# Two chained transformer blocks on one core: pipelined heads and TensorE squares in the first, earlier gates, a first sparse score and a last projection by halves in the second

## The chip, the cores and the metric

The kernel runs on one core of a Trainium2 chip. The metric is the device time of one execution in microseconds (us), lower is better. Before the change three runs took 2322.05, 2326.41 and 2326.66 us, median 2326.41. The engines are TensorE (PE in the profile), ScalarE (ACT), VectorE (DVE), GpSimd (POOL) and SyncE (SP), each with its own queue in program order; they meet at semaphores.

## The reference

256 tokens of width 1024 pass through two layers of a first block and then two layers of a second block, all in fp32.

```
first block, each of 2 layers:
  h = rms_norm(x); one projection h @ w_in gives
    an LRU branch (conv, two sigmoid gates, a scan over time, gelu),
    8 heads of forgetting attention (fox), 4 heads of retention (rotary q and k, decay, norm)
  x += rms_norm(concat(lru, fox, ret) @ w_out)
  x += rms_norm(cross_attention(rms_norm(x), memory))      # 4 heads
  x += rms_norm(swiglu(rms_norm(x)))                        # hidden 2816
second block, each of 2 layers:
  x += 0.5 * swiglu(rms_norm(x))
  h = rms_norm(x); h @ w_in gives
    8 heads of sparse attention (NSA: compressed, selected, window, gated by sigmoid(24 logits)),
    4 heads of stick-breaking attention, 4 heads of window attention with sinks,
    3 x 1024 branch gates
  x += (sum of 3 gated branches) @ w_out
  x += 0.5 * swiglu(rms_norm(x))
```

## The kernel before

**Weights.** All weights come as one stream of 664 half slots of 128 x 1024 fp32 (512 KB), two per slot of 1024 x 256. SyncE loads a half into one of 4 ring buffers `raw`; ScalarE rounds it to fp32r (`w_hi`, L837, in `split_hi`); VectorE takes the rest (`w_lo`, L1351, in `split_lo`). `ahead(name)` in the programs of ScalarE and VectorE splits the slot that follows `name` in the stream; where it stands among the other work of that engine decides when the slot is ready. TensorE multiplies a half with `products` (L286): for each 128 x 128 tile three matmuls of 256 columns (hi x hi, hi x lo, lo x hi), so 24 a half and 48 a slot. After its last matmul a half raises `half_used`, which frees the ring buffer.

**Norms.** `norm_in` takes the new x by four pairs of 128-row tiles. For pair b VectorE updates x (`update`: L1409 twice, then L1413, x + sq), ScalarE makes `xn_hi` (L855, L856) and the square of x (L848), VectorE makes `xn_lo` (L1373). GpSimd adds the squares of pairs 1, 2 and 3 onto pair 0 (`add_squares`, L1964); when the sum is there TensorE makes the mean (`mean_square`, L335, two matmuls that show as 4 instructions). The slot that follows (`fed`) starts with the pairs that are there. There are five such norms, before cross attention and swiglu in both layers of the first block and before the first swiglu of the second block, beside others.

**First block, mixer.** TensorE runs the projections; the slot `f` gives 8 forget logits, from which ScalarE and VectorE compute their sums over time (`f8`; L1518 to L1528). TensorE turns them into biases (L415), then runs `rv`. GpSimd makes the angles, and ScalarE the sine after `ly` and the cosine (L934) after `f` (layer 0 only). Then `conv` (L1543, L1548), the LRU gates (L432), eight memory slots `ck0` to `cv3` (keys and values of cross attention), placed between: the LRU chain (L984 to L1574), rotary (L439, L1585 to L1588), the loop over fox heads (`fox_scores` L451, `fox_softmax` L1600 to L1466, `fox_turn` L363, `fox_values` L358, L359) and retention (L482, L1626, L490 on). In `fox_softmax` VectorE waits for the exponentials of ScalarE (L1008, L1009) inside each head. Retention does one head after the other: scores, decay, values. Then four slots `wo`.

**Second block.** After the projections TensorE runs 18 fill matmuls (`keep_busy`, L294), 24 gate logits as 16 matmuls of 24 columns (L652), `cmp_turn` (L601), the slot `sv` (`project(9)`), `cmp_out_of(1)` (L614), `stick_scores` 0 and 1, and the loop over NSA heads (L696 to L727): each step has scores, one slot of the branch gates (`bg`), turn and values. ScalarE makes the gates' sigmoid (L1208) after the slot `sv`. At the end four slots `up` give three branches by four column pairs; VectorE multiplies and adds them (L1919 to L1924), and gives `merged_hi` and `merged_lo` for pair b (L1329, L1361). After 24 fill matmuls the four slots `wo0` to `wo3` follow, one column pair each over all 8 row tiles; `add` (L1932) adds a finished pair, from PSUM, to x.

The order of the work is written out by hand in the five programs; nothing plans it.

Of the kernel before, what the change touches and what calls it, by code (L numbers as in the profile page):

```python
# [15 lines left out]
P = 128  # L16
D = 1024
KT = D // P
S = 256
# [80 lines left out]
def build(nc, A):  # L100
# [7 lines left out]
    def sb_at(name, shape, dt, offset):  # L108
# [85 lines left out]
    gate24 = stat[:, 4:6, 0:24]  # L194

# [55 lines left out]
    kc_mean, kc_root, kc_normed, gate_made, gate_ready, gates_out = (  # L251
        sig(n) for n in ("kc_mean", "kc_root", "kc_normed", "gate_made", "gate_ready", "gates_out"))
# [16 lines left out]

    def norm_no(L, k, add=False):  # L270

        n = 1 + 6 * L + 2 * k + add if L < DEPTH else 1 + 6 * DEPTH + 3 * (L - DEPTH) + k
        return n if n > 1 else 0

    added = [norm_no(L, k, True) for L in range(DEPTH) for k in range(3)]

    def sums_before(n):

        return 3 * n - len([a for a in added if a < n])


    def tensor_program():
# [22 lines left out]
        def slot_T(name, out, hi, lo, cts=(0, 1), fed=None, second=None):  # L305

            for half, r in halves(name):
                if half and second:
                    T.wait_ge(*second)
                if fed is not None:  # L310
                    for k in range(HK):
                        if k % 2 == 0:
                            T.wait_ge(*in_lo.at(4 * fed + 2 * half + k // 2 + 1))
                        for ct in cts:
                            m = products(out[:, ct, :], tile(r, k, slice(ct * P, (ct + 1) * P)),
                                         [t[:, half * HK + k, :] for t in (hi, lo)], half == 0 and k == 0 and ct == cts[0])
                else:
# [4 lines left out]
                m.then_inc(*half_used.next())  # L322

        def slot_rows(name, out, hi, lo):
            for half, r in halves(name):
                for rt in range(ST):
# [39 lines left out]
        def ffn(f, fed, n):  # L366
            slot_T((f, "gate", 0), dense[0], xn_hi, xn_lo, fed=fed)
            norm_scale(n)
# [21 lines left out]
        for L in range(DEPTH):  # L390
# [75 lines left out]
            for n in range(8 + 2):  # L466
# [11 lines left out]
            for h in range(4):  # L478
                q, k = lru_a[head_rows(h), h // 2, :], lru_t[head_rows(h), h // 2, :]
                b = flat(acc[h % 2])  # L480
                T.wait_ge(*(ret_decayed.at(4 * L + h - 1) if h >= 2 else scores_read.at(head + 8)))
# [4 lines left out]
                T.wait_ge(*ret_decayed.at(4 * L + h + 1))  # L486
                causal_values(acc[2 + h // 2][head_rows(h), 0, :], lambda kt: proj[:, 12, kt, h * HD:(h + 1) * HD],
                              probT[h % 2][:, 0, :]).then_inc(*ret_values.next())
# [14 lines left out]
            for n in range(4):  # L503
                T.wait_ge(*(cross_out.at(4 * L + n - 1) if n >= 2 else kv_out.at(8 * L + 7 + n)))
                slot_T(at(f"cq{n}"), dense[n % 2], xn_hi, xn_lo, fed=3 * L + 1 if n == 0 else None)
                if n == 0:
                    norm_scale(norm_no(L, 1))
# [46 lines left out]
        for L in range(DEPTH, 2 * DEPTH):  # L554
# [4 lines left out]
            def project(n, form=slot_T):  # L559
# [7 lines left out]
                form(at(("nq0", "nq1", "nk", "nc", "sq", "sk", "wq", None, "nv", "sv")[n]), dense[n % 2], xn_hi, xn_lo)  # L567
# [78 lines left out]
            keep_busy(18, mix_rows.at(3 * l + 1), dense[1])  # L646
            T.wait_ge(*wg_ready.at(l + 1))
            T.wait_ge(*head_root.at(5 * l + 5))
            wg = small_2("w_gate").rearrange("p (k n) -> p k n", k=KT)
            for rt in range(2):  # L650
                for k in range(KT):
                    m = T.matmul(bank[4][:, rt * 24:(rt + 1) * 24], x[:, k, rt * P:(rt + 1) * P], wg[:, k, :],  # L652
                                 start=k == 0, stop=k == KT - 1)
# [28 lines left out]
            stick_scores(1)  # L682
            T.wait_ge(*kc_normed.at(l + 1))
            T.wait_ge(*cmp_out.at(2 * l + 2))
            T.wait_ge(*gate_ready.at(l + 1))
            T.wait_ge(*head_normed.at(5 * l + 5))

            def nsa_scores(h):
# [3 lines left out]
                if h >= 1:  # L692
                    T.wait_ge(*scores_read.at(head + h))
                for b in range(2):
# [8 lines left out]
            def nsa_turn(h):  # L703
                lg = logit[h % 2]
                T.wait_ge(*probs_made.at(head + h + 1))
                if h >= 1:
                    T.wait_ge(*probT_made.at(head + h))
                    T.wait_ge(*probT_made2.at(8 * l + h))
                for b in range(2):
# [4 lines left out]
            def nsa_values(h):  # L714
# [6 lines left out]
                if h >= 1:  # L721
                    T.wait_ge(*y_made.at(16 + 12 * l + h))
                for b in range(2):
# [5 lines left out]

            slot = 0  # L730
            for n in range(8 + 2):
                if n < 8:
                    nsa_scores(n)
                if n not in (0, 6, 9):
                    gate_slot(slot)
                    slot += 1
                elif n:
# [91 lines left out]
    def scalar_program():  # L829
# [86 lines left out]
        def memory_step(name):  # L916
# [14 lines left out]
            elif name in ("ly", "f"):  # L931
                n = ("ly", "f").index(name)
# [3 lines left out]
        for L in range(DEPTH):  # L936
# [20 lines left out]
            AC.wait_ge(*f_read.at(L + 1))  # L957
            AC.activation(f8[:, 1, :], f8[:, 0, :], ACT.Abs, bias=small[0:8, SM1["fox_b"]]).then_inc(*f_abs.next())
            AC.wait_ge(*f_abs.last())
            AC.activation(f8[:, 1, :], f8[:, 1, :], ACT.Exp, scale=-1.0).then_inc(*f_exp.next())  # L960
            AC.wait_ge(*f_exp.last())
# [1260 lines left out]
```

## Time and profile before

| what | value |
|---|---|
| median of 3 runs | 2326.41 us (2322.05 to 2326.66) |
| profiled execution | 2324.44 us, its span 2323.1 us |
| mean granted TensorE clock | 0.973 |
| PE busy | 2197.7 us, 95% of the span |
| DVE, ACT, POOL busy | 1419.0, 1131.7, 91.0 us |
| HBM traffic | 360.36 MB, mean 155 GB/s |

A time read in the profile is from the span's start. Busy time of PE is modelled, so that 95% doesn't mean that TensorE runs at its peak. In the views of waits, a row names the instruction that waited and what ended the wait. In the chain, each piece ends by releasing the next one.

### The profile page before, as it was taken

The numbers are of one execution on the slowest core, as the hardware profiler recorded it, in microseconds if no ns is written. First come the engines' busy times: TensorE is split into PE (matmuls) and PEld (weight loads), VectorE is DVE, ScalarE is ACT, GpSimd is POOL, SyncE is SP. The second block draws the span as 40 slices with busy tenths as digits, with TensorE's granted clock in tenths as the row PEclk, the third lists the DMA queues.
The fourth block names the chain that finished last, engine by engine and source line by source line (L and its number), as shares of the span: only waits on it lengthen the run. The fifth ranks groups of instructions, "written<-read, shape, count | busy, mean of one in ns | idle before, by whom it ended". The sixth has DMA issues, their size and how long they took to land.

```text
span 2323.1 us, 41302 instructions
## 1 busy us (share of the span) xinstructions
PE 2197.7 (95%) x17598; PEld 2104.4 (91%) x17598; DVE 1419.0 (61%) x2152; ACT 1131.7 (49%) x1758; POOL 91.0 (4%) x95
## 2 busy tenths in 40 slices
PE   6989899999889999999999999999999999999999
PEld 6868789999768899989998888999999998889999
DVE  5654665556547566566667567655666574667664
ACT  4554444434545444444546556444444455555443
POOL 4100000000000000000000000000000000000000
PEclk9989999999979999999999899999999988999999
DMA  5423246645324345646555224555566552234654
GB/s 208 151 85 128 83 148 205 211 145 177 114 73 134 108 160 186 199 156 197 190 195 175 81 91 131 171 187 189 176 197 204 179 171 91 91 122 151 195 192 159
DMA packets 98487, 360.36 MB, mean 155 GB/s; under 512 B 11136, under 2 KB 11149, under 8 KB 97920
## 3 DMA queue, kind: packets, MB, share of 16 engines
q1 hardware_dynamic: 96192, 349.22, 45.7%
q0 software_dynamic: 1680, 5.35, 0.7%
q8 instruction: 139, 2.28, 0.4%
q10 hardware_dynamic: 432, 3.15, 0.3%
q14 instruction: 44, 0.36, 0.0%
HBM read 356.61 MB, written 3.43 MB: 155 GB/s over the span
## 4 chain that ended last, share of the span: by engine, by line
PE 77%; DVE 14%; ACT 6%; issue 2%; DMA 0%; POOL 0%; DVEq 0%; ACTq 0%; SPq 0%; POOLq 0%
PE bank L286 68%; DVE w_lo L1351 4%; ACT w_hi L837 2%; PE bank L358 1%; DVE x L1413 1%; DVE xn_lo L1373 1%; DVE sq L1409 1%; PE bank L696 1%; PE bank L363 1%; DVE sq L1919 1%; PE bank L359 1%; DVE rinv L1731 1%; PE bank L354 0%; DMA raw<-in_stream 0%; DVE rinv L1403 0%
## 5 line engine op out<-in xcount | busy, mean ns | idle before, releaser
L1351 DVE TENSOR_TENSOR w_lo<-raw,w_hi 128x1024 fp32r<-128x1024 f32 x664 | 797.3, 1236 | 425.1 <-ACT w_hi L837 424.7
L286 PE MATMUL bank<-xn_hi,w_hi 128*128 128x256 f32 x3168 | 897.3, 283 | 53.4 <-DVE xn_lo L1373 43.2
L286 PE MATMUL bank<-xn_lo,w_hi 128*128 128x256 f32 x3168 | 887.4, 280 | 0.0
L286 PE MATMUL bank<-xn_hi,w_lo 128*128 128x256 f32 x3168 | 887.2, 280 | 0.0
L837 ACT ACTIVATE w_hi<-raw 128x1024 fp32r<-128x1024 f32 x664 | 673.6, 1051 | 255.1 <-PE bank L286 243.6
L286 PEld LDWEIGHTS bank<-xn_hi,w_hi 128*128 128x128 f32 x3168 | 602.4, 190 | 64.8 <-issue 51.0
L286 PEld LDWEIGHTS bank<-xn_hi,w_lo 128*128 128x128 f32 x3168 | 602.4, 190 | 0.0
L286 PEld LDWEIGHTS bank<-xn_lo,w_hi 128*128 128x128 f32 x3168 | 600.4, 190 | 1.1 <-issue 1.0
L286 PE MATMUL bank<-hid_hi,w_lo 128*128 128x256 f32 x1056 | 294.1, 279 | 0.0
L286 PE MATMUL bank<-hid_hi,w_hi 128*128 128x256 f32 x1056 | 294.1, 278 | 0.0
L286 PE MATMUL bank<-hid_lo,w_hi 128*128 128x256 f32 x1056 | 294.1, 278 | 0.0
L286 PEld LDWEIGHTS bank<-hid_hi,w_lo 128*128 128x128 f32 x1056 | 199.7, 189 | 0.0
L286 PEld LDWEIGHTS bank<-hid_hi,w_hi 128*128 128x128 f32 x1056 | 199.0, 188 | 0.0
L286 PEld LDWEIGHTS bank<-hid_lo,w_hi 128*128 128x128 f32 x1056 | 198.2, 188 | 0.0
L893 ACT ACTIVATE hid_hi<-act_t 128x512 fp32r<-128x512 f32 x66 | 41.8, 634 | 193.0 <-DVE act_t L1427 193.0
L889 ACT ACTIVATE act_t<-act_t 128x512 f32<-128x512 f32 x66 | 41.9, 635 | 184.9 <-DVE act_t L1422 184.9
L286 PE MATMUL bank<-y_hi,w_hi 128*128 128x256 f32 x384 | 107.3, 279 | 5.4 <-DVE y_lo L1361 4.6
L286 PE MATMUL bank<-y_hi,w_lo 128*128 128x256 f32 x384 | 106.4, 277 | 0.0
L286 PE MATMUL bank<-y_lo,w_hi 128*128 128x256 f32 x384 | 106.4, 277 | 0.0
L1964 POOL TENSOR_TENSOR sq<-sq 128x512 f32<-128x512 f32 x39 | 54.4, 1394 | 1319.0 <-ACT sq L848 1318.1
L286 PEld LDWEIGHTS bank<-y_hi,w_hi 128*128 128x128 f32 x384 | 72.1, 188 | 7.5 <-DVE y_lo L1361 3.6
L1361 DVE TENSOR_TENSOR hid_lo<-act_t,hid_hi 128x512 fp32r<-128x512 f32 x66 | 45.8, 693 | 50.8 <-ACT hid_hi L893 50.8
(351 smaller groups left out, 2854.6 us busy)
## 6 DMA issues: line engine op xcount, KB each, us to landing
raw<-in_stream SPq DMA_DIRECT2D x664, 512.0 KB, 4.2
skew<-vec POOLq DMA_DIRECT2D x12, 192.0 KB, 3.9
table<-skew POOLq DMA_DIRECT2D x1, 1408.0 KB, 7.3
con<-in_con ACTq DMA_DIRECT2D x1, 1029.0 KB, 14.9
x<-in_x ACTq DMA_DIRECT2D x1, 1024.0 KB, 6.8
xn<-in_mem ACTq DMA_DIRECT2D x1, 1024.0 KB, 11.5
out<-x SPq DMA_DIRECT2D x4, 256.0 KB, 3.3
logit<-in_small POOLq DMA_DIRECT2D x3, 288.5 KB, 3.0
```

Of the source, the lines that this page charges most:

```text
L286: m = T.matmul(out, a, b, start=first and j == 0, stop=True, skip_group_check=True)
L358: T.matmul(out, v_of(0), pT[:, 0:S], start=first, stop=False, skip_group_check=True)
L359: return T.matmul(out[:, P:S], v_of(1), pT[:, S:S + P], start=False, stop=last, skip_group_check=True)
L363: m = T.transpose(dst[:, to * P:(to + 1) * P], src[:, frm:frm + P], c("ident"))
L696: T.matmul(out[:, LATE], q[:, P:S], k, start=True, stop=True)
L837: AC.activation(w_hi[m % RING], raw[m % RING], ACT.Copy).then_inc(*hi_done.next())
L889: AC.activation(act_t, act_t, ACT.Silu).then_inc(*silu_made.next())
L893: AC.activation(hid_hi[:, 2 * j:2 * j + 2, :], act_t, ACT.Copy).then_inc(*hid_hi_made.next())
L1351: V.tensor_tensor(w_lo[m % RING], raw[m % RING], w_hi[m % RING].bitcast(F32), ALU.subtract).then_inc(*lo_done.next())
L1361: V.tensor_tensor(lo, src, hi.bitcast(F32), ALU.subtract).then_inc(*to.next())
L1373: m = V.scalar_tensor_tensor(xn_lo[:, k, :], x[:, k, :], gain[:, k:k + 1], xn_hi[:, k, :].bitcast(F32), ALU.mult, ALU.subtract)
L1964: G.tensor_tensor(sq[:, 0:2, :], sq[:, 0:2, :], sq[:, pair_of(b), :], ALU.add).then_inc(*summed.next())
```

## The change

```diff
+    gates_T = act_t[0:24, 0, :]
+    wo_out = [misc[0], misc[1], dense[1], acc[0]]
+    by_pairs = [norm_no(L, k) for L in range(DEPTH) for k in (1, 2)] + [norm_no(DEPTH, 0)]
...
+        def pair_of_squares(n, b):
+            T.wait_ge(*squared.at(4 * n + b + 1))
+            for k in (2 * b, 2 * b + 1):
+                m = T.matmul(misc[0][:, 0, :], avg, sq[:, k, :], start=k == 0, stop=k == KT - 1, skip_group_check=True)
+            if b == 3:
+                m.then_inc(*mean_made.next())
...      # slot_T, fed: after each second k
+                        if k % 2 and squares is not None:
+                            pair_of_squares(squares, 2 * half + k // 2)
...      # first block, TensorE
-            for n in range(2):
-                T.matmul(flat(misc[n]), c("rot"), flat(proj[:, 4 + n, :, :]), start=True, stop=True
-                         ).then_inc(*rot_turned.next())
...      # end of each step of the fox loop
+                if n >= 8:
+                    T.wait_ge(*scores_read.at(head + n - 1))
+                    T.matmul(flat(acc[n - 8]), c("rot"), flat(proj[:, n - 4, :, :]), start=True, stop=True
+                             ).then_inc(*rot_turned.next())
+            memory_slot(5)
             T.wait_ge(*rot_made.at(2 * L + 2))
...
-                if h == 0:
-                    memory_slot(5)
+            for h in range(4 + 1):
+                if h < 4:
+                    retention_scores(h)
+                if h:
+                    T.wait_ge(*ret_decayed.at(4 * L + h))
+                    causal_values(... of head h - 1 ...)
...      # first block, ScalarE
-            elif name in ("ly", "f"):
+            elif name in ("ly", "rv"):         # the cosine, now after out_rows(12, "rv")
...      # Abs, Exp and Ln of "lam" now right behind those of f8, before ahead("fv1")
+            memory_slot(2)
             AC.wait_ge(*lru_made.at(L + 1))
             AC.activation(y_hi[:, 0:2, :], lru_h, ACT.Copy).then_inc(*lru_hi.next())
-            memory_slot(2)
+            memory_slot(3)
...      # first block, VectorE: "lam" before conv; ahead("ck1") after root_in; the low half of the LRU output
...      # after the first head's maximum; rotary after the fox loop; ahead("cv2") after the four decays
             for n in range(8 + 2):
                 if n < 8:
-                    fox_softmax(n)
-                if n in (1, 4):
-                    ahead(at("ck3" if n == 1 else "cv0"))
+                    fox_max(n)
+                if n == 0:
+                    low_half(y_lo[:, 0:2, :], lru_h, y_hi[:, 0:2, :], lru_hi.at(L + 1), own)
+                if 1 <= n < 9:
+                    fox_weights(n - 1)
+                if n in (1, 3, 6):
+                    ahead(at({1: "ck3", 3: "cv0", 6: "cv1"}[n]))
...      # second block, TensorE
-            keep_busy(18, mix_rows.at(3 * l + 1), dense[1])
-            T.wait_ge(*head_root.at(5 * l + 5))
+            T.wait_ge(*head_root.at(5 * l + 4))
-            for rt in range(2):
-                for k in range(KT):
-                    m = T.matmul(bank[4][:, rt * 24:(rt + 1) * 24], x[:, k, rt * P:(rt + 1) * P], wg[:, k, :], ...)
+            for k in range(KT):
+                m = T.matmul(bank[5][0:24, 0:S], wg[:, k, :], x[:, k, :], start=k == 0, stop=k == KT - 1)
             m.then_inc(*gate_made.next())
             cmp_turn(1)
-            project(9, slot_rows)
-            cmp_out_of(1)
             stick_scores(0)
-            stick_scores(1)
+            T.wait_ge(*gate_copied.at(l + 1))
+            # two transposes of gates_T into bank[5]; gate_turned
+            project(9, slot_rows, between=lambda: nsa_scores(0))      # between the halves of "sv"
+            cmp_out_of(1)
+            stick_scores(1)
-            for n in range(8 + 2):
+            for n in range(1, 8 + 2):
...      # second block, ScalarE: copy of the gates, ahead("sv"), sigmoid, stick_exp(0), nsa_exps(0),
...      # then out_rows(9, "sv"), cmp_out_of(1), stick_exp(1) and the loop from n = 1
...      # second block, the last projection
-            keep_busy(24, None, misc[1])
-            T.wait_ge(*merged.at(4 * l + 3))
-            for b in range(4):
-                slot_T(at(f"wo{b}"), acc[b], merged_in_hi, merged_in_lo, second=merged.at(4 * l + 4) if b == 0 else None)
+            for i in range(4):
+                T.wait_ge(*(merged.at(4 * l + 2), branch_read.at(4 * l + 3), merged.at(4 * l + 4), merged.at(4 * l + 4))[i])
+                for part, r in halves(at(f"wo{i}")):
+                    b, half = 2 * (i % 2) + part, i // 2
+                    for ct in range(2):
+                        for k in range(HK):
+                            m = products(wo_out[b][:, ct, :], ... [t[:, half * HK + k, :] for t in (merged_in_hi, merged_in_lo)] ...)
+                    m.then_inc(*half_used.next())
...      # VectorE: ahead("wo0") between branch_read and the sums of the last branch; ScalarE and VectorE:
...      # ahead("wo1"), ahead("wo2"), beside(0), ahead("wo3"), beside(1), beside(2)
...      # GpSimd: no add_squares for the norms in by_pairs; host: w_out_2 laid out by row halves
```

## Rows read from the trace of the kernel before

**Rows 1.** The profile's page: granted TensorE clock in 40 slices, in tenths.
```profile
PEclk9989999999979999999999899999999988999999
```
**Rows 2.** Waits of PE over the span: us in total, times, longest.
```profile
PE bank L286 <- DVE xn_lo L1373: 43.2, 19, 16.6
PE bank L286 <- DVE w_lo L1351: 22.0, 20, 3.0
```
**Rows 3.** The chain through a norm, 315 to 334 us: start, us, what.
```profile
314.44 0.69 DVE x L1413
315.13 0.79 DVE xn_lo L1373 x2
315.92 0.80 DVE sq L1409 x2
...
316.74 1.76 DVE x L1413
...
322.82 2.97 PE bank L286 x24
325.79 0.88 PE bank L335 x4
```
**Rows 4.** POOL's timeline, 311 to 323 us: start, us, idle before in brackets.
```profile
316.69 1.27 POOL L1964 TENSOR_TENSOR sq<-sq 128x512 f32<-128x512 f32 x1 [7.88 <-ACT sq L848]
```
**Rows 5.** Timelines of ACT and PE, 84 to 89 us.
```profile
84.61 0.42 ACT L934 ACTIVATE cos<-probT 128x256 f32<-128x256 f32 x1 [7.43 <-POOL probT L2005]
...
88.74 0.58 PE L286 MATMUL bank<-w_hi,xn_hi 128*128 128x256 f32 x1 [5.20 <-DVE act_t L1518]
```
**Rows 6.** ACT's timeline, 109 to 125 us.
```profile
113.81 1.28 ACT L986 ACT_TABLE_LOAD   x1
```
**Rows 7.** The chain through layer 0's mixer, 80 to 335 us.
```profile
108.07 0.84 ACT proj L952 x2
...
135.02 0.60 DVE lru L1585
...
208.13 20.02 PE bank L286 x168
```
**Rows 8.** PE's timeline in the fox loop, 163 to 170 us.
```profile
163.65 0.55 PE L363 MATMUL bank<-con,logit 128*128 128x128 f32 x3
...
164.92 0.92 PE L451 MATMUL bank<-proj 64*128 64x256 f32 x4
166.47 0.55 PE L363 MATMUL bank<-con,logit 128*128 128x128 f32 x3 [0.63 <-DVE logit L1466]
```
**Rows 9.** DVE's timeline in the fox loop, 166.6 to 170 us.
```profile
166.66 0.42 DVE L1600 CUSTOM_DVE_ANT_0 logit<-bank,xn 128x256 f32<-128x256 f32 x1
...
168.56 0.17 DVE L1606 RECIPROCAL stat<-stat 128x2 f32<-128x2 f32 x1 [1.06 <-ACT logit L1009]
...
169.22 0.42 DVE L1600 CUSTOM_DVE_ANT_0 logit<-bank,xn 128x256 f32<-128x256 f32 x1
```
**Rows 10.** Windows: us, busy of PE, PEld, DVE, ACT, POOL, granted clock, DMA share, GB/s.
```profile
134.00:174.00 40.00, 34.24 (x177) 27.34 (x178) 22.30 (x78) 17.75 (x51) 0.00 (x0) 0.79 0.25 79
...
1273.00:1300.00 27.00, 23.65 (x150) 21.64 (x148) 9.02 (x29) 14.70 (x33) 0.00 (x0) 0.79 0.30 100
```
**Rows 11.** PE's timeline of the fill, then the chain, 1270 to 1301 us.
```profile
1273.91 2.12 PE L294 MATMUL bank<-ones 128*128 128x256 bf16 x18
...
1276.58 5.30 PE bank L652 x32
...
1282.23 7.25 PE bank L286 x48
...
1299.89 1.15 PE bank L286 x4
```
**Rows 12.** PE's waits at 1448 to 1481 us, and all instructions of L1932 (ns min/median/max).
```profile
PE bank L286 <- DVE merged_lo L1361: 3.3, 1, 3.3
...
L1932 DVE TENSOR_TENSOR x<-x,bank x8: 677/681/683, 1465.4 to 2139.1; 128x512 f32<-128x512 f32 x8
```

More of the change, by code:

```diff
@@ L321, in slot_T, with slot_rows @@
                                          [t[:, half * HK + k, :] for t in (hi, lo)], half == 0 and k == 0 and ct == cts[0])
-                m.then_inc(*half_used.next())
-        def slot_rows(name, out, hi, lo):
+                    m.then_inc(*half_used.next())
+        def slot_rows(name, out, hi, lo, between=None):
             for half, r in halves(name):
+                if half and between:
+                    between()
                 for rt in range(ST):
@@ L366, in ffn @@
         def ffn(f, fed, n):
-            slot_T((f, "gate", 0), dense[0], xn_hi, xn_lo, fed=fed)
-            norm_scale(n)
+            slot_T((f, "gate", 0), dense[0], xn_hi, xn_lo, fed=fed, squares=n if n in by_pairs else None)
+            if n not in by_pairs:
+                norm_scale(n)
             for j in range(FB):
@@ L681, in tensor_program @@
             stick_scores(0)
-            stick_scores(1)
[L683 to L686, printed above, removed]
+            T.wait_ge(*gate_copied.at(l + 1))
+            for rt in range(2):
+                m = T.transpose(bank[5][:, S + rt * 24:S + (rt + 1) * 24], gates_T[:, rt * P:(rt + 1) * P],
+                                c("ident")[0:24, 0:24])
+            m.then_inc(*gate_turned.next())
             def nsa_scores(h):
@@ L1330, in scalar_program @@
             beside = next_in(3 * L + 2, small_2("ffn2"))
-            for b in range(4):
-                if b:
-                    ahead(at(f"wo{b}"))
-                    beside(b - 1)
+            ahead(at("wo1"))
+            ahead(at("wo2"))
+            beside(0)
+            ahead(at("wo3"))
+            beside(1)
+            beside(2)
             beside = next_in(3 * (L + 1), small_2("ffn1"), small_ready.at(L + 1)) if l + 1 < DEPTH else lambda b: None
@@ L1617, in vector_program @@
                     low_half(y_lo[:, 2 + h, :], misc[h % 2][:, 0, :], y_hi[:, 2 + h, :], y_hi_made.at(8 * L + h + 1), y_made)
+            for n in range(2):
+                rotary(n)
             for h in range(4):
@@ L1920, in vector_program @@
                 m.then_inc(*branch_read.next())
+                if b == 3:
+                    ahead(at("wo0"))
                 V.wait_ge(*branch_read.last())
@@ L1924, in vector_program @@
                 V.tensor_tensor(t3[0], t3[0], t3[2], ALU.add).then_inc(*branch_sum.next())
-                ahead(at(("up1", "up2", "up3", "wo0")[b]))
+                if b < 3:
+                    ahead(at(f"up{b + 1}"))
                 V.wait_ge(*branch_sum.last())
@@ L1930, in add @@
             def add(b):
-                V.wait_ge(*slot_end(at(f"wo{b}")))
-                V.tensor_tensor(x[:, pair_of(b), :], x[:, pair_of(b), :], acc[b], ALU.add).then_inc(*x_updated.next())
+                V.wait_ge(*wo_end(l, b))
+                V.tensor_tensor(x[:, pair_of(b), :], x[:, pair_of(b), :], wo_out[b], ALU.add).then_inc(*x_updated.next())
             beside = next_in(3 * L + 2, small_2("ffn2"), add)
-            for b in range(4):
-                if b:
-                    ahead(at(f"wo{b}"))
-                    beside(b - 1)
+            ahead(at("wo1"))
+            ahead(at("wo2"))
+            beside(0)
+            ahead(at("wo3"))
+            beside(1)
+            beside(2)
             last = half_update(DEPTH + 2 * l + 1)
@@ L2113, in dense, with dense_by_halves @@
             put(pair(w[:, c:c + COLS]))
+    def dense_by_halves(w):
+        blocks = [pair(w[:, c:c + COLS]) for c in range(0, w.shape[1], COLS)]
+        for half in range(2):
+            rows = [b[:, half * SLOT // 2:(half + 1) * SLOT // 2] for b in blocks]
+            put(np.concatenate(rows[0:2], 1))
+            put(np.concatenate(rows[2:4], 1))
     def ffn(gate, up, down):
```

142 lines of the change are left out of this document (80 added, 62 removed).

## The prediction

> **What bounds the kernel now.** I read the page first. The clock line shows TensorE at its high level (2.4 GHz) nearly everywhere; the slices under 9 hold stretches at 1.2 GHz [rows 1]. TensorE is the bound: in dense stretches 168 matmuls of 256 columns take 20.02 us [rows 7], 0.119 each, so a slot of 48 costs 5.7 us, and the 15,936 matmuls of the 664 halves cost about 1,900 of the 2,323 us. No part of that is removed. What a change can win is the rest, where TensorE waits or runs small matmuls. The view of waits names the largest: 43.2 us behind `xn_lo` (norms) and 22.0 us behind `w_lo` (a slot not yet split) [rows 2]. Then I read the chain and timelines at each place the diff touches, and the granted clock there. The sum is made against the profiled execution, 2324.44 us (span 2323.1), which lies within the runs, 2 us under their median 2326.41.
>
> **1. Squares on TensorE, five norms.** Before, VectorE sets the pace of a tail: per pair 0.80 (L1409), the add into x, 0.79 (`xn_lo`). The add took 0.69 for an early pair and 1.76 for the later two [rows 3]; the slow one began at 316.74, 0.05 us after a GpSimd add of squares had begun for 1.27 us [rows 4]. Two such adds a norm: 2 x 1.07 = 2.1 us that go with GpSimd's work. The Trainium skill (SBUF — State Buffer, "Who interferes with whom") says that a VectorE instruction with two SBUF inputs is blocked while a GpSimd instruction that reads SBUF runs; by this rule, which these rows bear out, both slow adds become fast.
> Added: per pair two matmuls of squares; the two of the old mean took 0.88 us [rows 3], and they go, so the count in the tail rises by three pairs, 2.6 us, in what was idle time. VectorE then needs 0.80 + 0.69 + 0.79 = 2.3 us a pair, TensorE 12 x 0.119 + 0.88 = 2.3 as well: the cover is used up. Four pairs of 2.3 make 9.2 us from pair 0 to the mean; before it was from 316.0 (where pair 0's `xn_lo` is done) to 325.79 + 0.88 = 326.7, 10.7 us. Gain 1.5 each, 7.5 for five. Bounds: 2.1 + 0.5 each if TensorE keeps up better, 13; at 1.2 GHz TensorE needs 4.6 a pair and loses (a rival below). I add 1 for a stretch at 1.2 GHz that a busier tail may avoid. **Gain 8.5.**
>
> **2. First block's mixer.** (a) Layer 0 only: ScalarE waits 7.43 us for the cosine's angle, splits the next slot late, and TensorE waits 5.20 behind the forget logits [rows 5]. With the cosine moved this wait goes, but TensorE next waits for the same chain of `f8` (three table loads and small operations), then for `conv`, which has the `lam` operations put before it. I keep half: gain 2.8 (bounds 0 and 5.2). Layer 1 pays about 0.4 for the `lam` operations in that chain.
> (b) From the end of `rv` (108.07) to the output slots (208.13) layer 0 takes 100 us [rows 7]. In the LRU chain two table loads of 1.28 us [rows 6] leave ScalarE's critical path, since `lam` shares the sets of `f8`; with `ahead` for `ck2` and `ck3` earlier, TensorE's waits for `w_lo` before them (1.5 and 2.9, part of the 22.0 in [rows 2]) go. Rotary, on VectorE from 135.02 to about 138.8 while TensorE has nothing, moves behind memory slot 5, which covers it (5.7 against 4): 3.8 us. Retention's pairing takes off some 2 us. Low half, copies and reorderings: about 1. A simple sum is 1.5 + 2.9 + 3.8 + 2 + 1 = 11 with an earlier end of the LRU chain of some 3 more.
> (c) Against it: the new fox loop. Before, VectorE did maximum, wait for the exponentials (1.06 idle), weights: one head in 2.56 us (166.66 to 169.22) [rows 9], and TensorE's turn, values and next scores (163.65 to 165.84, 2.2 us) ran beside it [rows 8]. After, VectorE takes `fox_max(n)` then `fox_weights(n-1)`, but TensorE issues scores n+1 only behind the turn of head n-1, which waits for those weights. The cycle is scores, maximum 0.9, weights 0.65, turn, values: 2.2 + 1.55 + 0.1 = 3.9 us. The 1.06 idle is won and the overlap lost, 1.3 us a head, for about five heads with no memory slot beside them: -6.5 less the shorter start, net -3. So at full clock a layer wins 11 + 3 - 3 = 11.
> (d) The clock. The stretch 134 to 174 has a granted 0.79 [rows 10]: that is some 17 of 40 us at 1.2 GHz, one memory slot among them. Before it fell TensorE had done single heads with waits between. The new cycle has TensorE busy 2.2 of 3.9 us; the old one, at 2.2 of 2.6 to 2.9, kept 2.4 GHz. At 1.2 GHz the cycle is 4.4 + 1.65 = 6 us, so four heads cost 8 us and the slot behind them more. I take 4 off each layer: 7.5 (bounds 2 and 12). **Gain of part 2: 2.8 - 0.4 + 15 = 17.4.**
>
> **3. Second block's gates and first sparse scores, two layers.** Before, from the fill at 1273.91 (2.1 us) to the first gate slot at 1299.89: fill, gates 5.30 (16 matmuls, begun at 1276.58), slot `sv` 7.25, `cmp_out`, stick scores, ScalarE's sigmoid with its table load, scores 0, VectorE's maximum, scores 1 [rows 11]. The granted clock there is 0.79 [rows 10]. After: gates begin at about 1274.0; 8 matmuls of 256 fp32 columns at 0.44 (two of them took 0.88 [rows 3]) make 3.5; turn, stick scores and transposes 1.3; first half of `sv` 2.85, scores 0 1.8, second half 2.85: 1286.3. ScalarE's sigmoid, and VectorE's maximum of head 0, lie beside the second half. What is late next: `stick_scores(1)` needs the rows of `sv`, which ScalarE copies only after the exponentials of head 0 (2.5): TensorE waits about 2. Then 0.6, scores 1 1.8: gate slot 0 begins at 1291.2. That is 8.7 earlier, plus 1 since it runs at full clock: 9.7. If the clock falls here as before, 2 to 3 less. **Gain 8.5 a layer, 17** (bounds 5 and 10.5 each).
>
> **4. Last projection by halves, two layers.** Before: 24 fill matmuls (2.5 us), half a slot, a wait of 3.3 for the last `merged_lo` [rows 12], then from 1458.4 seven halves, 20.0 and 1.7 for a stretch at 1.2 GHz, to 1480.1. So `up3` ended at 1458.4 - 3.3 - 2.85 - 2.5 = 1449.8. After: `wo0` needs pairs 0 and 1 only and starts some 0.3 behind `up3`, when it is split; four halves (11.4) cover the sums of the last pair, which `ahead("wo0")` now delays by 2.4 on VectorE. The projection ends at 1450.1 + 8 x 2.85 = 1472.9: 7.2 earlier. But the four results come 2.85 apart at the end and VectorE must do add, two splits and `xn_lo` in that time; I see `xn_lo` of pair 3 about 1 late. And GpSimd still adds squares here: 0.68 for L1932 [rows 12], 1.76 if it is slowed as L1413 was [rows 3], up to twice. **Gain 5 a layer, 10** (bounds 3.5 and 7).
> The same page of the Trainium skill says that an instruction with at most one SBUF input doesn't contend; L1932 adds from PSUM, so by that rule its adds stay at 0.68 and the gain would be 6.3 a layer. No row of L1932 beside a GpSimd add shows it.
>
> **Sum.** 8.5 + 17.4 + 17 + 10 = 53: 2324.4 - 53 = 2271.5; taken halfway to the median, **2273 us**.
>
> **Rivals.**
> - *The head loops run at 1.2 GHz throughout.* Part 2 gives 5, part 3 11, part 4 9, part 1 8: 33, so 2292. For it: 0.79 in both stretches [rows 10], and the longer cycle. Against: two waits that came before the fall are gone. Chance 0.25.
> - *The clock holds everywhere.* Part 2 26, part 3 20, part 4 13, part 1 11: 70, so 2256. Chance 0.15.
> - *The heads aren't pipelined by the change, and the fox cycle is worse than I reckon* (4.5 us at the high level, both blocks; memory slots late behind it): part 2 gives 0 and part 3 half: 27, so 2299. Chance 0.06.
> - *Slower: the squares on TensorE become the bound of the tails.* At 1.2 GHz a pair costs TensorE 12 x 0.238 + 1.76 = 4.6 us against 3.35 that VectorE needed before (0.80 + 1.76 + 0.79); it decides from the point where TensorE needs over 3.35, so only with the clock down. A tail then takes 18.4 + against 10.7: five lose 38, and with parts 2 to 4 at their lows (4 + 10 + 7) the end is 2324 + 17 = 2341. For it: idle time inside tails before. Against: 50 fill matmuls still run ahead of each, and the new tail has no idle time. Chance 0.03.
>
> **How the numbers follow.** Forecast 0.51 (2263 to 2284). With the next two the range is **2253 to 2300**, about 85%. 0.2% of this kernel is 5 us, what its measurement can tell from none: slower by more 0.04 (the last rival and what I overlook), within it 0.02, faster 0.94.
>
> **What would show it.** Part 1: L1413 at 0.69 throughout those five tails, L335's rows there gone or spread, `xn_lo` waits down by 10 us or more. Part 2: the wait behind L1518 gone; from `rv` to `wo0` 90 to 94 us in place of 100; turns (L363) 3.9 us apart or 6 at 1.2 GHz. If they are 2.6 apart, my cycle is wrong and the time is lower. Part 3: 18 us from the first gate matmul's predecessor to gate slot 0, a wait of 2 before `stick_scores(1)`. Part 4: no wait behind `merged_lo`, a new one of about 1 behind `xn_lo`. The forecast is wrong if the granted clock in the fox loop falls below 0.7, or if a gained microsecond is met by a split that comes later.

## The result, and the profile after

| kernel | runs | median us | lowest to highest |
|---|---|---|---|
| before | 4 | 2324.23 | 2320.61 to 2326.66 |
| after | 4 | 2264.53 | 2257.53 to 2268.34 |

The ratio is 0.9745 with a 95% interval of 0.9704 to 0.9786: faster by 59.7 us in the medians. I had put 2273 and 2253 to 2300. A second set of six runs gave 2265.3 and 0.9748. Ratios and intervals here leave out runs more than 1.5% above the fastest of their kernel, which takes out one run of `splits_beside`, its profiled one, and two of the kernel before beside it.

The profiled execution after the change took 2268.34 us, its span 2267.0; the clock line has two slices under 9 in place of five [rows 1].

```profile
PEclk9989999999989999999999999999999999999999
```

PE's waits (us, times, longest), against [rows 2], with one more row of the kernel before ahead of them:

```profile
PE bank L363 <- DVE logit L1466: 10.3, 11, 1.8
```
```profile
PE bank L296 <- DVE xn_lo L1429: 28.0, 13, 16.6
PE bank L387 <- DVE logit L1522: 21.0, 12, 3.4
PE bank L296 <- DVE w_lo L1407: 14.8, 22, 1.5
PE bank L296 <- DVE y_lo L1417: 4.6, 4, 1.4
...
PE bank L704 <- ACT proj L1210: 2.8, 2, 1.4
```

The norm wait fell from 43.2 to 28.0 and the split wait from 22.0 to 14.8. What has grown is the wait before a fox head's turn for its weights: L363 behind L1466 had 10.3, and L387 behind L1522, the same two instructions, has 21.0. L704 behind L1210 is the wait ahead of `stick_scores(1)` that part 3 was to bring, 1.4 a layer.

**Part 1**, the chain through the same norm as [rows 3]:

```profile
305.66 0.69 DVE x L1469
306.35 0.80 DVE xn_lo L1429 x2
307.15 0.14 issue
307.29 1.63 PE bank L296 x12
308.92 0.86 PE bank L319 x4
309.78 1.42 PE bank L296 x12
311.19 0.87 PE bank L319 x4
...
315.80 0.88 PE bank L319 x4
```

The add into x is 0.69, and the chain now stays on TensorE: 1.42 + 0.87 = 2.3 us a pair, as worked out. VectorE sets the pace no longer.

**Part 2**, PE's timeline in the fox loop (start, us, instruction, idle before), against [rows 8]:

```profile
148.92 0.49 PE L387 MATMUL bank<-con,logit 128*128 128x128 f32 x3
...
150.13 0.92 PE L473 MATMUL bank<-proj 64*128 64x256 f32 x4
152.64 0.55 PE L387 MATMUL bank<-con,logit 128*128 128x128 f32 x3 [1.59 <-DVE logit L1522]
...
153.91 0.92 PE L473 MATMUL bank<-proj 64*128 64x256 f32 x4
156.42 0.55 PE L387 MATMUL bank<-con,logit 128*128 128x128 f32 x3 [1.59 <-DVE logit L1522]
...
162.02 0.55 PE L387 MATMUL bank<-con,logit 128*128 128x128 f32 x3 [3.41 <-DVE logit L1522]
```

Turns come 3.72 and 3.78 us apart, and each waits 1.59: scores, then maximum and weights on VectorE with TensorE idle, then the turn. It is the cycle of 3.9 of the prediction. The next turn is 5.60 behind and waits 3.41, since VectorE splits `cv2` ahead of that head's weights. It does so in both layers, and the prediction has no term for it. Before, the last four intervals were 2.1 to 2.9.

**Part 3**, chain from the last piece of head 0's exponentials, against [rows 11]:

```profile
1262.44 2.44 ACT logit L1282 x12
1264.88 0.73 ACT proj L1210 x2
...
1265.65 0.48 PE bank L704
...
1267.68 5.67 PE bank L296 x48
```

The exponentials (2.44) stand ahead of the copy of `sv`'s rows, which is what `stick_scores(1)` waits for. Gate slot 0 starts at 1267.68, 17.0 behind the first gate matmul (1250.7), where the prediction has 17.2 (1274.0 to 1291.2).

**Part 4**, VectorE and GpSimd behind the last projection, against [rows 12]:

```profile
1439.74 0.68 DVE L1997 TENSOR_TENSOR x<-x,bank 128x512 f32<-128x512 f32 x1
1441.40 1.00 DVE L1429 SCALAR_TENSOR_TENSOR xn_lo<-x,small,xn_hi 128x256 fp32r<-128x256 f32 x2 [0.98 <-ACT xn_hi L902]
1442.32 0.68 DVE L1997 TENSOR_TENSOR x<-x,bank 128x512 f32<-128x512 f32 x1
```
```profile
1440.39 1.31 POOL L2031 TENSOR_TENSOR sq<-sq 128x512 f32<-128x512 f32 x1
1441.96 1.58 POOL L2031 TENSOR_TENSOR sq<-sq 128x512 f32<-128x512 f32 x1 [0.26 <-ACT sq L894]
```

The add from PSUM stays at 0.68 though GpSimd adds beside it from 1441.96 on. Here the trace agrees with the Trainium skill (SBUF — State Buffer, "Who interferes with whom"), which exempts an instruction with at most one SBUF input. `xn_lo` has two, and took 1.00 in place of 0.88.

**Two spacings of dense matmuls.** Before the parts can be compared, one thing that no part of the change touches must be taken out. Windows of two swiglus in the trace after (us, busy of PE with its count, PEld, DVE, ACT, POOL, granted clock, DMA share, GB/s):

```profile
340.00:440.00 100.00, 100.00 (x885) 100.00 (x884) 62.85 (x65) 47.64 (x56) 5.28 (x10) 1.00 0.66 214
840.00:940.00 100.00, 100.00 (x852) 100.00 (x851) 57.53 (x58) 44.82 (x52) 0.00 (x0) 1.00 0.60 194
```

The same instructions at the same granted clock: 885 or 852 in 100 us, 0.1133 or 0.1178 us each. One spacing holds for a whole swiglu, and which it is changes from profile to profile: the first block's first norm and swiglu take 192.5 to 194.0 us or 198.4 to 199.6 (one of 14 profiles, that of `redraw`, lay between). In the stages counted the trace before has 7,764 matmuls at the wide spacing, the trace after 8,892, worth 5 us against the change; over all profiles it was 3,300 to 11,316, or 36 us. The table compares stages (between two splits on VectorE, at the same slots in every kernel) with 0.0045 us taken off for each matmul at the wide spacing; I call that equal pace.

```
us at equal pace         before  after  again  no_squares no_mixer no_gates no_halves
mixer, layer 0            189.0  183.5  187.0     182.4     188.7    183.7    182.9
mixer, layer 1            183.9  174.0  174.9     174.8     180.5    176.3    173.9
cross attention, layer 0   74.3   71.3   71.3      72.6      71.4     71.3     71.4
cross attention, layer 1   71.6   71.3   71.3      71.5      71.3     71.3     71.3
norm + swiglu, layer 0    193.4  192.2  192.2     193.5      192.2   192.2    192.2
norm + swiglu, layer 1    193.4  192.1  192.1     193.4      192.2   192.2    192.2
first swiglu, block 2     194.1  192.7  192.7     194.3      192.8   192.8    192.7
gates + NSA, layer 0      148.9  138.8  139.6     137.9      138.4   148.2    138.4
gates + NSA, layer 1      152.3  137.9  142.0     142.0      138.6   151.7    137.8
up3, wo, norm, layer 0     57.0   51.7   51.5      51.5       52.7    52.3     56.2
up3, wo, norm, layer 1     56.8   52.0   51.9      51.8       51.5    51.1     56.9
projections, layer 1       85.6   80.8   80.6      85.9       80.4    80.4     80.6
```

Where no edit touches them, the stages of cross attention and the swiglus agree within 0.2. The others hold stretches at 1.2 GHz of changing length and spread more with one and the same code. The mixer of layer 0 takes 182.4 to 187.0: where the granted clock from 128 to 175 us is 0.64 (`again` and two further profiles) it takes 186.7 to 187.0, where it is 0.75 to 0.85 it takes 182.4 to 184.4. Gates and NSA of the change take 137.8 to 138.8 with no dense matmul at 1.2 GHz, and 139.6 to 142.8 with 3 to 29 of them. The 5 us in the last line are of that kind too. So a difference of some 2 us in one such stage of one trace shows nothing, and the parts are priced by means over traces.

### The profile page after: what moved, and what is told of

It reads as the page before. It is cut to its first block, busy times and chain, and to the rows that moved or that the text cites. A ratio compares the mean times of both kernels' runs of the same rounds, so it can differ in the third digit from the quotient of the medians.

```text
span 2267.0 us, 41174 instructions
## 1 busy us (share of the span) xinstructions
PE 2171.6 (96%) x17546; PEld 2074.3 (91%) x17546; DVE 1403.9 (62%) x2152; ACT 1128.0 (50%) x1757; POOL 72.8 (3%) x80
## 4 chain that ended last, share of the span: by engine, by line
PE 81%; DVE 12%; ACT 5%; issue 1%; DMA 0%; ACTq 0%; DVEq 0%; SPq 0%
PE bank L296 70%; DVE w_lo L1407 3%; PE bank L382 2%; ACT w_hi L883 1%; DVE rinv L1794 1%; PE bank L387 1%; PE bank L319 1%; PE bank L383 1%; PE bank L728 1%; DVE xn_lo L1429 1%; DVE x L1469 1%; DVE sq L1465 1%; DVE sq L1981 1%; PE bank L378 0%; DMA raw<-in_stream 0%
## 5 line engine op out<-in xcount | busy, mean ns | idle before, releaser
L296 PEld LDWEIGHTS bank<-y_hi,w_hi 128*128 128x128 f32 x384 | 72.1, 188 | 7.5 <-DVE y_lo L1417 3.6
L1483 DVE TENSOR_TENSOR act_t<-act_t,bank 128x512 f32<-128x512 f32 x66 | 45.4, 688 | 52.8 <-PE bank L296 52.8
```

The source lines that it names most:

```text
L296: m = T.matmul(out, a, b, start=first and j == 0, stop=True, skip_group_check=True)
L1483: V.tensor_tensor(act_t, act_t, dense[1], ALU.mult).then_inc(*up_read.next())
```

## The experiments

All but `writing_gpsimd` were timed, four to six runs each beside the kernel before on the same chip. The first four shared a chip, then four, then three.

**Each part undone: again, no_squares, no_mixer, no_gates, no_halves.** Part 1 undone is

```diff
-    by_pairs = [norm_no(L, k) for L in range(DEPTH) for k in (1, 2)] + [norm_no(DEPTH, 0)]
+    by_pairs = []
```

with `add_squares` back on GpSimd; the others take back the hunks of their part.

> The changed kernel once more, as the mark for the three beside it. All theories: 2262 to 2268 us, 57 to 61 below the kernel before. A theory on TensorE's pace (dense stretches run at one of two spacings of matmuls at the same granted clock, and which one is chance): the totals of the two spacings will be other than in the first trace, and single runs of one kernel will lie up to 10 us apart.

2265.3 us (2253.08 to 2269.6), 53.8 under the median of the kernel before beside it (2319.12), where 57 to 61 was expected; single runs lie 16.5 apart, not 10. The wide spacing had 7,332 matmuls, other than the 8,892 of the first trace, as expected.

> The changed kernel without part 1: GpSimd adds the squares again in all five norms, TensorE takes one mean of two matmuls. My theory: part 1 is worth 7.7 us by the traces (predicted 8.5), so about 2272; L1469 back to 1.76 for two adds of each tail, the tail from pair 0 to the mean back from 9.0 to 10.3 us. Rival (the tails are bound by the arrival of matmuls on TensorE, or the gain was clock luck): under 3 us slower than the changed kernel.

2270.8, ratio to before 0.9783 (0.9742 to 0.9825). At equal pace 1.3 + 0.2 + 1.3 + 1.3 + 1.6 = 5.7 us in the five tails, where 7.7 was expected. In the same norm two adds into x are back at 1.77 and 1.76, as expected, and the chain is back on VectorE. The whole runs, 5.5 apart with intervals that overlap, don't decide against the rival's 3; the stages do.

> The changed kernel with the first block's mixer as before (part 2 undone: cosine after f, lam, order of the slots, serial heads, rotary ahead of the heads, retention by single heads). My theory: parts add up, so 17 us slower than the changed kernel, about 2282 (predicted 17.4). Rival: most of it was chance of the clock in the layer-1 mixer; then under 9 us.

2270.2, ratio 0.9800 (0.9750 to 0.9849). The runs can't decide; the stages can. Means of the traces with the mixer of the change against the two without it: layer 0 184.7 against 188.9, layer 1 174.6 against 182.2, so 11.9 us (here and below the means also take in the experiments further down that leave the stage alone). That is between the theory's 17 and the rival's 9. With two traces on one side and the spread told above, it is known to a few us.

> The changed kernel with the second block's gates, first sparse scores and fill as before (part 3 undone). My theory: 21 us slower than the changed kernel by the two traces, 17 predicted, so 2282 to 2286. Rival (2 x 1 to 2 of it is the clock, which falls here by chance): 17 or less.

2287.5, ratio 0.9850 (0.9810 to 0.9889), 22 us slower than `again`. At equal pace 138.8 against 148.6 and 139.1 against 152.0: 9.8 + 12.9 = 22.7 (the means leave out `scores_ahead`, `splits_beside` and `paced`; with the first two it is 22).

> The changed kernel without part 4: 24 fill matmuls, wo by column pairs in the layers of the second block. My theory: 5 us a layer, 10 in all (predicted 10, the traces 10.6): the stretch from up3 to the third gate slot 57 in place of 52 us, about 2275. Rival (what was won before the wo slots is paid behind them in the norm): 4 us or less.

2287.4, ratio 0.9872 (0.9808 to 0.9936); its runs lay 26 us apart. At equal pace 51.9 against 56.6 and 51.6 against 56.9: 10.0. The theory stands by the stages, the runs' larger difference is not the part's.

**The fox loop: serial_heads.**

```diff
-                    fox_max(n)
-                if n == 0: low_half(...)
-                if 1 <= n < 9:
-                    fox_weights(n - 1)
+                    fox_max(n)
+                    if n == 0: low_half(...)
+                    fox_weights(n)
```

> The changed kernel, but VectorE takes the weights of a fox head right behind its maximum, as before (TensorE's and ScalarE's programs untouched). My theory: the pipelined order costs the heads 1.2 us each since the scores of the next head start only behind the turn of the last, so serial heads come 2.5 to 2.9 us apart in place of 3.8, five a layer with no slot beside them: the two mixers 10 to 13 us shorter together, about 2253. Rival A (the heads' distance is set by something else, ScalarE or the memory slots): turns stay 3.8 apart and the time stays within 3 us of the changed kernel. Rival B (serial heads wait for the exponentials): slower by 1 us a head, 10 to 16 us.

2259.3 us, ratio 0.9745 (0.9688 to 0.9801). At equal pace the mixers take 179.8 and 174.3, 4.9 and 0.3 less than the means. By whole runs it isn't shown faster than the change. Heads with neither a slot nor a split beside them come 1.6 to 2.9 apart, but the gain is half of the 10 to 13. VectorE's timeline in layer 1 shows where the rest is:

```profile
614.92 0.17 DVE L1664 RECIPROCAL stat<-stat 128x2 f32<-128x2 f32 x1 [1.05 <-ACT logit L1060]
615.13 0.55 DVE L1522 TENSOR_SCALAR logit<-logit,stat 128x256 f32<-128x256 f32 x2
615.59 2.35 DVE L1407 TENSOR_TENSOR w_lo<-raw,w_hi 128x1024 fp32r<-128x1024 f32 x2
617.86 0.42 DVE L1655 CUSTOM_DVE_ANT_0 logit<-bank,xn 128x256 f32<-128x256 f32 x1
...
619.76 0.17 DVE L1664 RECIPROCAL stat<-stat 128x2 f32<-128x2 f32 x1 [1.05 <-ACT logit L1060]
...
623.38 0.17 DVE L1664 RECIPROCAL stat<-stat 128x2 f32<-128x2 f32 x1 [2.12 <-ACT logit L1060]
```

Where a split (2.35) or ScalarE's share of one stands among the heads, the serial order adds the wait for the exponentials (1.05 to 2.12) to it, and the clock fell in that stretch (the turn at 620.56 waits 2.64 and takes 0.90 in place of 0.55). The pipelined order hides that wait but loses the overlap with TensorE. Each order is the better one at some heads.

**scores_ahead.**

```diff
+            fox_scores(0)
             for n in range(8 + 2):
-                if n < 8:
-                    fox_scores(n)
+                if n < 7:
+                    fox_scores(n + 1)
```

> The changed kernel, with one change on TensorE: in each step of the fox loop it makes the scores of head n+1, not n, ahead of the turn of head n-1. My theory: this gives back the overlap that the pipelining lost; VectorE then goes maximum 0.9, weights 0.65 and waits for the turn (0.55 and 0.1 to 0.2 for semaphores), so heads 2.3 to 2.6 us apart in place of 3.8; five a layer without a slot beside them: 12 to 15 us less in both mixers together, about 2251. Rival (TensorE's small matmuls or ScalarE bound the cycle): over 3.3 apart and under 6 us won.

2268.4, ratio 0.9789 (0.9735 to 0.9842). PE's timeline:

```profile
146.20 0.49 PE L387 MATMUL bank<-con,logit 128*128 128x128 f32 x3
...
148.39 0.55 PE L387 MATMUL bank<-con,logit 128*128 128x128 f32 x3
...
152.06 0.55 PE L387 MATMUL bank<-con,logit 128*128 128x128 f32 x3 [1.49 <-DVE logit L1523]
...
157.66 0.90 PE L387 MATMUL bank<-con,logit 128*128 128x128 f32 x3 [4.25 <-DVE logit L1523]
```

Heads with no split between them come 2.2 apart, three of the seven intervals in each layer, so the cycle was right. But then VectorE splits `cv2` inside the loop, TensorE waits 4.25 and goes on at 1.2 GHz (0.90 for a turn). The mixers: 181.4 and 176.0, 1.8 us less in all, not 12, and within the spread of these stages. Once the heads are quick, the splits among them set the pace of the loop.

**splits_beside.**

```diff
-                if n in (1, 3, 6):
-                    ahead(at({1: "ck3", 3: "cv0", 6: "cv1"}[n]))
+                if n in (1, 4):
+                    ahead(at("ck3" if n == 1 else "cv0"))
...
             for n in range(2):
                 rotary(n)
+            ahead(at("cv1"))
```

and the same moves on ScalarE, over scores_ahead.

> scores_ahead (scores one head ahead on TensorE), and the split of cv1 moved from head 3 to head 4, where TensorE runs a memory slot and ScalarE and VectorE stand idle for 4 us; the split of cv2 moved from head 6 to behind the fox loop and rotary. In scores_ahead heads came 2.2 us apart, but TensorE waited 4.25 us before the turn of head 6 (VectorE stood 1.83 behind w_hi and 2.36 in the split of cv2) and ran on at 1.2 GHz. My theory: that wait and the low clock behind it go (4.3 + 2), and 1 to 2 from the other split: L0 mixer 176 and L1 mixer 170 us at the quicker spacing of matmuls, against 184 and 175 in the changed kernel (means of the traces), 12 us in all, about 2253. Rival (the split comes late for cv2 or retention and is paid there): under 4 us below the changed kernel.

```profile
152.31 0.55 PE L387 MATMUL bank<-con,logit 128*128 128x128 f32 x3 [1.49 <-DVE logit L1522]
...
154.56 0.56 PE L387 MATMUL bank<-con,logit 128*128 128x128 f32 x3 [0.91 <-DVE logit L1522]
```

The wait of 4.25 is 0.91. The one interval with a split left in it is still 3.7, and in layer 0 the clock still falls behind this wait. The mixers take 176.6 and 169.6 at equal pace where 176 and 170 were expected: 13.0 us under the means of the change. The median of six runs is 2252.0 (2238.98 to 2278.28), and that of the five that the ratio takes 2250.93, the lowest here, with a ratio of 0.9731 (0.9681 to 0.9780). That interval holds the 0.9745 and 0.9748 of the change itself: by whole runs it isn't shown faster. By the two stages it is: 176.6 and 169.6 lie under all eight traces with the change's mixer (182.4 and 173.2 at the least), and `paced`, with the same loop, has 177.3 and 168.4. This profile (span 2277.0) had 11,316 matmuls at the wide spacing, the most of all, and 5 us at 1.2 GHz in the projections of the last layer.

**GpSimd beside the tails: reading_gpsimd, writing_gpsimd.**

```diff
+                for _ in range(4):
+                    G.tensor_tensor(scratch, ones, ones, ALU.add)      # reading_gpsimd
+                    G.memset(scratch, 1.0)                             # writing_gpsimd
```

> The changed kernel (squares on TensorE in the five norms), and GpSimd does idle work in them: for pairs 1 to 3 four adds 128x128 of a constant into a scratch tile, where it used to add squares; nothing waits for it. Theory (VectorE's add into x, with two SBUF inputs, is held up while GpSimd reads SBUF): the mean of L1469 (0.78 in the changed kernel, 1.23 with part 1 undone) goes back to 1.1 or more, tails last 10 us again in place of 9.0, 5 to 6 us in all. Rival (the tail was shortened because TensorE takes the sum itself, not by VectorE's add): the time stays within 2 us of the changed kernel at an equal pace of TensorE.

> As reading_gpsimd, but GpSimd only writes (four memsets of 128x128 for each pair) where that one had adds that read SBUF. The adds made each of the five tails 0.8 us longer at equal pace (L0 cross 71.3 to 72.1, L0 n3+swiglu 192.2 to 193.0, and alike in the others). Theory (GpSimd's reads hold up VectorE's two-input adds): 0.1 or less a tail. Rival (any work of GpSimd does): 0.5 or more a tail, as far as the memsets last.

With the reading adds 2265.1 us (ratio 0.9770, 0.9712 to 0.9827), the five stages are 0.8 us longer each (72.1, 72.1, 193.0, 193.0, 193.5): 4.1 us of the 5.7 that part 1 brings. The chain of its tail:

```profile
312.64 0.88 DVE x L1470
313.52 1.08 DVE xn_lo L1430 x2
314.60 0.80 DVE sq L1466 x2
315.42 0.69 DVE x L1470
316.12 1.09 DVE xn_lo L1430 x2
```

The add and `xn_lo`, both with two SBUF inputs, are slowed; `sq` (L1466), which reads PSUM, stays at 0.80; and the chain is back on VectorE. L1469's mean rose only to 0.82, not to the 1.1 that I had put: these adds of 128x128 leave gaps, and most of the price falls on `xn_lo`, which I had left out: in this tail 0.19 on the add and 0.28 + 0.29 on two pairs of `xn_lo`. With memsets (0.99 us for each pair) the stages are 71.3, 71.3, 192.1, 192.2, 192.7, those of the change to 0.1; its one run took 2266.8. The memsets are shorter than the adds (0.99 against 2.28 us for four), but the first four, from 310.77, lay over an add into x from 310.86, and that took 0.69. So it is adds that read SBUF that cost, not any work of GpSimd.

**The spacing: redraw, paced.**

```diff
                 if j:
                     T.wait_ge(*up_read.at(FB * f + j))
+                    keep_busy(1, None, misc[1])                        # redraw
+                else:
+                    keep_busy(1, None, misc[1])                        # paced, and ahead of nine other slots
```

> The changed kernel with one idle matmul (bf16, 256 columns) ahead of each up slot of the swiglus but the first, 60 in all: about 60 x 0.11 = 7 us more work. In all traces dense matmuls follow each other at 0.1133 or 0.1178 us at the same granted 2.4 GHz, one of the two for up to 180 us. Theory A (any matmul of another kind lets the pace be drawn anew): both spacings alternate within each swiglu, none keeps one for over 50 us, and the runs lie closer together, near 2264 + 7. Theory B (only a wait of TensorE draws anew): spacings stay for 180 us as before. Theory C (the idle matmul sets one of them): all slots behind one are alike, and the time is 2250 or 2280.

2256.3 us, 9 less than `again` with some 10 us more work, and its four runs lie within 1.6 us. Beside the kernel before, which ran faster that time too, its ratio is 0.9757 (0.9707 to 0.9807) against 0.9748, so it isn't shown faster. Each idle matmul costs a gap of 0.20 us and some four matmuls at 0.115 to 0.127 behind it; then the spacing is 0.1133 throughout, down slots included. (It isn't twelve at 0.1178, as my next expectation has it.) In 55 of the 60 cases the spacing was 0.1133 ahead of the idle matmul already; five times, at the first one of a swiglu, it was 0.1178 and changed. 3,300 matmuls at the wide spacing are left, from other stages. The window that was wide in the trace after (columns as there):

```profile
840.00:940.00 100.00, 100.00 (x882) 99.75 (x880) 59.23 (x60) 45.24 (x52) 0.00 (x0) 1.00 0.63 200
```

This is theory C with the quick spacing, as far as this place goes: behind the matmul nothing is wide, where in the 13 other profiles 42 of 78 swiglus are.

> splits_beside (2252, 2239 to 2278 in 6 runs), with one idle matmul (bf16, 256 columns) ahead of the first up slot of each swiglu and, in the other stages, ahead of fk0, fk1, ck0, cv1, wo1, cq1, co0 of the first block and nk and up0 of the second: 22 in all. In redraw every idle matmul was followed by about 12 matmuls at 0.1178 us and then 0.1133 until the next stall or small fp32 matmul, through the down slots too, and its four runs lay within 1.6 us. Theory (the idle matmul sets the quicker spacing): all swiglus at 0.1133 after their first 12 matmuls (192 to 193 us for those of the first block with their norm, 324 for the two in the middle), at most 3000 matmuls at 0.1178 in place of 4500 to 11300, runs within 10 us, median 2232 to 2238. Rival (it was chance, or needs an idle matmul every 11 us to hold): swiglus of 198 us come again, median 2248 to 2256, runs spread over 15 us or more.

2267.1 us (2264.0 to 2272.33), ratio 0.9742 (0.9715 to 0.9769) on another chip. (The idle matmuls were 24, not 22.) The theory falls in this form: four of the six swiglus are wide again, 7,944 matmuls in all. The trace tells three cases apart. Right behind small fp32 matmuls, as those of a norm's squares, the idle matmul sets nothing: of 13, 6 were followed by the quick spacing and 7 by the wide one. With dense matmuls or a wait ahead of it and the next dense matmul 0.04 us behind it, as in all 60 cases of `redraw`, all 10 were followed by the quick one; six of them stood between two dense slots and changed it from wide. Once, between two dense slots, the next dense matmul came 0.25 us behind it and the spacing went from quick to wide. PE's timeline, that case first and then one of the ten:

```profile
516.23 0.28 PE L304 MATMUL bank<-ones 128*128 128x256 bf16 x1
516.48 0.38 PE L296 MATMUL bank<-xn_hi,w_hi 128*128 128x256 f32 x1
```
```profile
522.24 0.28 PE L304 MATMUL bank<-ones 128*128 128x256 bf16 x1
522.28 0.37 PE L296 MATMUL bank<-xn_hi,w_hi 128*128 128x256 f32 x1
```

One case doesn't show that the gap is what matters; what TensorE's state is that tells them apart stays open. The two mixers kept their gain (177.3 and 168.4 at equal pace), but both projection stages of the second block had 5 to 6 us at 1.2 GHz. Over all profiles that came in 4 of 6 such stages with scores_ahead's loop and in 2 of 22 without; whether the loop has to do with it or chance, I can't tell.

## Why the prediction was right

| part | predicted | at equal pace, by undoing it |
|---|---|---|
| 1, squares | 8.5 | 5.7 |
| 2, mixer | 17.4 | 11.9 |
| 3, gates | 17 | 22.7 |
| 4, last projection | 10 | 10.0 |
| sum | 53 | 50.3 |

The profiled runs differ by 56.1: 50.3, 5 of the low clock that the trace before had in the projections of the last layer, 1.7 more in cross attention of layer 0 (74.3 against 72.6 in `no_squares`: the low clock in that norm's tail, under part 1), and some 5 by which these two traces differ more than the means in the mixers and gates, less 5 of the wider spacing. That 2273 came out near 2265 is in part luck: parts 1 and 2 were put 8.3 too high and part 3 5.7 too low.

- **Part 1.** The mechanism was right in each number: 0.69, and 2.3 us a pair on TensorE. Mis-sized was the gain of 1.5 a norm: it is 1.3, and 0.2 in cross attention of layer 1, which I didn't follow up. The 1 us for the clock isn't in the 5.7, since no tail of `no_squares` ran at 1.2 GHz. The trace before does have such a stretch in one of the five tails, that of cross attention in layer 0, whose mean ends at 248.6:

```profile
243.00:249.00 6.00, 5.89 (x34) 5.82 (x35) 3.66 (x4) 2.93 (x6) 1.47 (x1) 0.72 0.26 93
```

  A granted 0.72 in 6 us is 3.4 us at 1.2 GHz, which costs the 1.7 by which its stage is longer than that of `no_squares` (74.3 and 72.6). Whether squares on TensorE keep the clock up there or it was chance, one stretch in two traces doesn't show.
- **Part 2.** Mis-sized in layer 0: 4.2 where 10.3 was put, against 7.6 for 7.1 in layer 1. (The sum takes 7.5 a layer where its own 11 less 4 is 7.) Read from where TensorE starts the slots, at equal pace, as means over the eight traces with this mixer against the two without: `ck0` starts 3.6 earlier in layer 0, more than the 2.8 that I kept, and 0.1 later in layer 1. From `ck0` to `cv0` 7.1 and 11.4 are won and from `cv1` to `wo3` 3.0 and 4.7, so (b) brings 10.1 and 16.1 where I had 14; it was not tried by itself. From `cv0` to `cv1` 10.0 and 9.4 are lost, where net 3 and 4 for the clock made 7. The fox cycle of 3.9 is 3.8; what the price lacked is the head that waits for the split of `cv2` (5.6 us), and in three traces of layer 0 the low clock. So in layer 0 (b) and the new loop cancel, and the sign "90 to 94 us from `rv` to `wo0` in place of 100" failed there: counted from the end of `rv` to the first `wo` slot it is 96.3 before and 92.9 to 98.4 with the change. In layer 1 it is 97.4 before and 89.5 to 92.7.
- **Part 3.** The wait ahead of `stick_scores(1)` is 1.4 for 2. In layer 0 the gain is the 9.7 that I had worked out at full clock (my terms make gate slot 0 begin at 1290.7, not 1291.2, which is 0.5 more), so most of what I took off for the clock was wrong. In layer 1 the kernel with the old gates ran 39 and 52 dense matmuls of this stage at 1.2 GHz (0.21 us each), against 22 and 24 in layer 0; with the change there are none in most traces and up to 29 in others: 12.9.
- **Part 4.** 5.0 a layer as put, with two terms off in opposite directions. GpSimd's adds didn't slow the adds from PSUM, but VectorE stood 0.98 before each `xn_lo` of the last three pairs, the wait that I had put at 1 in all (2.9).

Of the rivals, the low clock throughout the head loops did not come in the profile after: some 55 us of it are at 1.2 GHz, against some 126 before. But in `again` and two more traces the granted clock in the loop of layer 0 is 0.64, under the 0.7 that I named as a sign of being wrong, and that mixer takes some 3 to 4 us longer. The rival is refuted as a rule, not for each run.

## What to carry over

Pipelining heads pays only if the other engine gets its next input ahead of the wait: here TensorE's scores one head further ahead turned 3.8 us a head into 2.2 where no split stands between, and only with the splits of weights moved beside a long slot did the stage get shorter. A reduction on an idle engine isn't free when it reads SBUF: GpSimd's adds cost VectorE more than two extra matmuls a pair cost TensorE. Compare variants of a few microseconds by stages in traces, first take out what differs in stages that none of them touches, and see how far one stage spreads with the same code.

## What the hardware showed unexpectedly

- Dense fp32r matmuls of 256 columns run at 0.1133 or 0.1178 us at one granted clock, for up to 180 us on end; in the swiglus the choice changes only where TensorE waits or runs other matmuls, and it decides 5.9 us of a norm and swiglu (192.5 or 198.4).
- One bf16 matmul with a dense one 0.04 us behind it was followed by the quick spacing in all 60 cases of `redraw` (five of them changes from wide) and in 10 of 10 in `paced` (six changes); right behind small fp32 matmuls in 6 of 13.
- A GpSimd add slows VectorE's instructions with two SBUF inputs: a pair of `xn_lo` 0.80 to 1.08 and the add into x 0.69 to 0.88 beside adds of 128x128, that add 0.69 to 1.77 beside one of 128x512. Memsets and adds from PSUM (0.68) show nothing of it.
